# Retention heads with tokens on the partitions: GroupNorm along the free axis, the output transposed afterwards, and the samples' outputs as column tiles

## What is computed

```python
qf = rope(q), kf = rope(k) * DK ** -0.5            # DK 256, per head
scores = einsum('bhid,bhjd->bhij', qc, kc) * decay  # prompt tokens
inner = einsum('bhij,bhje->bhie', scores, vc)       # o of the prompt, 512 x 512 per head
S_new = S * chunk_dec + k^T v                       # state, 256 x 512 per head
...                                                 # samples: 8 states of their own, o_b = q_b S_new_b
mu = mean(o, axis=-1); var = mean(square(o - mu), axis=-1)
o = (o - mu) * rsqrt(var + EPS) * gn_gain           # GroupNorm over the 512 channels of a head
ret_branch = (silu(g_ret) * o) @ w_ret_out
```

## Time and profile before

| | |
|---|---|
| three runs | 2767.01, 2780.33, 2778.76 us; median 2778.76 |
| the profiled execution | span 2784.4 us |
| PE busy | 2598.1 us, 93% of the span |
| DVE, POOL, ACT busy | 1435.8, 1404.3, 594.0 us |
| mean granted TensorE clock | 0.964 of full |
| chain that ended last | PE 72%, DVE 14%, the rest waits between engines |

### The profile page before, as it was taken

The page is one execution under the profiler, slowest core; times in us unless marked ns, Lnnn a source line. Parts: engine busy times, 40 slices in busy tenths (PEclk is TensorE's granted clock), DMA queues, the critical chain, the costliest instruction groups (busy, mean ns, idle before and its releaser), DMA issues.

```text
span 2784.4 us, 53033 instructions
## 1 busy us (share of the span) xinstructions
PE 2598.1 (93%) x20388; PEld 2551.3 (92%) x20388; DVE 1435.8 (52%) x1644; ACT 594.0 (21%) x825; POOL 1404.3 (50%) x845
## 2 busy tenths in 40 slices
PE   7999999987889999999999999899888899999997
PEld 7998989987889989999998989898788899999997
DVE  6656454587764553223256453646876745431333
ACT  2303030316161121001112121213161611110111
POOL 4252526244456656666653525252455566566664
PEclk9999999999999999999999989999999999999999
DMA  4435353422222222232236252524222222222222
GB/s 156 168 122 164 121 160 118 159 72 68 65 78 89 92 76 92 86 96 91 88 131 199 89 189 91 191 92 163 62 73 72 74 92 89 76 89 93 91 87 87
DMA packets 113015, 298.52 MB, mean 107 GB/s; under 512 B 11681, under 2 KB 12449, under 8 KB 112865
## 3 DMA queue, kind: packets, MB, share of 16 engines
q1 hardware_dynamic: 60480, 199.78, 22.4%
q10 hardware_dynamic: 52384, 96.56, 10.4%
HBM read 255.92 MB, written 40.38 MB: 106 GB/s over the span
## 4 chain that ended last, share of the span: by engine, by line
PE 72%; DVE 14%; DVEq 7%; issue 3%; ACT 2%; ACTq 1%; DMA 1%; POOL 0%; POOLq 0%
PE proj L299 63%; PE aux L469 3%; DVEq L1011 2%; DVE scratch L829 2%; PE aux L460 1%; PE aux L450 1%; DVEq L828 1%; DVE scratch L775 1%; PE aux L417 1%; DVE scratch L913 1%; DVE scratch L917 1%; DMA scratch<-v_rows 1%; DVE scratch L780 1%; ACTq L1269 1%; DVE scratch L638 1%
## 5 line engine op out<-in xcount | busy, mean ns | idle before, releaser
L285 POOL TENSOR_SCALAR w_high<-w_raw 128x1024 fp32r<-128x1024 f32 (+3 forms) x420 | 438.0, 1043 | 1294.5 <-PE proj L299 1290.2
L287 POOL TENSOR_TENSOR w_low<-w_raw,w_high 128x1024 fp32r<-128x1024 f32 (+3 forms) x420 | 965.9, 2300 | 62.2 <-issue 1.5
L299 PE MATMUL proj<-x_high,w_high 128*128 128x260 f32 x4096 | 855.2, 291 | 97.0 <-DVE scratch L895 34.6
L299 PE MATMUL proj<-x_high,w_low 128*128 128x260 f32 x4096 | 841.5, 288 | 0.0
L299 PE MATMUL proj<-x_low,w_high 128*128 128x260 f32 x4096 | 840.4, 287 | 0.0
L299 PEld LDWEIGHTS proj<-x_high,w_high 128*128 128x128 f32 x4096 | 650.4, 194 | 109.9 <-issue 52.5
L299 PE MATMUL proj<-split_scratch,w_high 128*128 128x260 f32 x4000 | 655.4, 286 | 43.5 <-DVE scratch L802 17.1
L299 PEld LDWEIGHTS proj<-x_high,w_low 128*128 128x128 f32 x4096 | 648.3, 193 | 0.0
L299 PEld LDWEIGHTS proj<-x_low,w_high 128*128 128x128 f32 x4096 | 647.7, 193 | 0.0
L299 PEld LDWEIGHTS proj<-split_scratch,w_high 128*128 128x128 f32 x4000 | 556.4, 191 | 51.0 <-DVE scratch L802 18.3
L299 PE MATMUL proj<-split_scratch,w_low 128*128 128x260 f32 x2000 | 406.2, 285 | 0.0
(11 more groups left out here) (142 smaller groups left out, 2086.5 us busy)
## 6 DMA issues: line engine op xcount, KB each, us to landing
w_raw<-in_wstream SPq DMA_DIRECT2D x252, 512.0 KB, 3.3
scratch<-in_sret ACTq DMA_DIRECT2D x64, 512.0 KB, 6.3
out_ret_s<-scratch ACTq DMA_DIRECT2D x64, 512.0 KB, 6.4
w_raw<-in_wstream SPq DMA_DIRECT2D x72, 448.0 KB, 3.2
w_raw<-in_wstream SPq DMA_DIRECT2D x48, 384.0 KB, 3.1
scratch<-v_rows ACTq DMA_DIRECT2D x64, 256.0 KB, 5.3
w_raw<-in_wstream SPq DMA_DIRECT2D x48, 320.0 KB, 2.9
out_ret_p<-scratch ACTq DMA_DIRECT2D x8, 512.0 KB, 3.1
```

The costliest lines, as they stand in the source:

```text
L285: pool.tensor_scalar(WH[:, j, w], WR[:, j, w], 1.0, 0.0, ALU.mult, ALU.add)
L287: pool.tensor_tensor(WL[:, j, w], WR[:, j, w], WH[:, j, w].bitcast(F32), ALU.subtract).then_inc(s["w_split"], 1)
L299: m = pe.matmul(out, wt[:, w, blk * P:(blk + 1) * P], x[xi], start=first and n == 0, stop=last and n == 2)
```

## The change

Within a head, o is now made token-major. `attend(i)` takes the scores as weights and v as the streaming operand, so the 128 tokens of block i stand on the partitions and the 512 channels on the free axis. ACT copies each block to `OT`. The GroupNorm sums are then sums along the free axis: DVE's `bn_stats` and `bn_aggr` give mean and variance of each token, ACT takes the root of five columns, and DVE normalises `OT` with two per-partition scalars. `out_by_channel` transposes the result back on PE, behind the first two q tiles of the next head, and `outs_gated` multiplies it with the gate straight out of PSUM. The matrix of ones, the centring, the squares and the 128x520 reciprocal are gone.

The samples' outputs are made in two rounds of four. Each sample's q stands alone in one column of a 32-column block of zeros (`QZ`); that block is the stationary operand, the state streams past it (512 columns), and the four samples of a round write four 32-partition quarters of one bank.

Around it the order changes: `ret_out` stands behind the v tiles, with `sample_v` (transposes of the samples' v) ahead of it; `sample_out(0)` follows `ret_out`, and `sample_out(1)` stands behind the last gate (in head 0 behind `gate(2)` and at the very end). DVE makes the states of the first round between the tiles of `ret_out`. Four x tiles instead of two come ahead of the layer's last `ret_out`, and their convolutions stand between its tiles. Each bank of `aux` has its own semaphore for being free. Cut to its core:

```diff
-X_EARLY = 2
+X_EARLY = 4
...
-BANK = [0, 1, 2, 3, 0, 1, 2, 3, 0, 1, 2, 0, 1, 2, 0, 1, 2]
+N_VS, N_SC, N_TK, N_TV, N_AT, N_ST, N_OS, N_OT = 0, 1, 5, 7, 11, 15, 17, 18
+BANK = [0, 1, 2, 0, 1, 2, 0, 1, 2, 0, 1, 2, 0, 1, 2, 0, 1, 3, 2, 0, 1, 2]
...
+                def out_by_channel(hh):
+                    pe.wait_ge(s["o_norm"], hh * (TT + 1) + (TT + 1))
+                    aux_begin(N_OS, hh)
+                    for e in range(VT):
+                        m = pe.transpose(AUX[:, BANK[N_OS], e * P:(e + 1) * P],
+                                         OT[:, TT, e * P:(e + 1) * P], ID[:])
+                    m.then_inc(s["aux_mm"], 1)
+                    for e in range(VT):
+                        aux_begin(N_OT + e, hh)
+                        for i in range(TT):
+                            m = pe.transpose(AUX[:, BANK[N_OT + e], i * P:(i + 1) * P],
+                                             OT[:, i, e * P:(e + 1) * P], ID[:])
+                        m.then_inc(s["aux_mm"], 1)
...
+                    def attend(i):
+                        aux_begin(N_AT + i, hh)
+                        for j in range(i + 1):
+                            at = ST_OFF[j] + (i - j) * P
+                            for n, (a, b) in enumerate(((STH, VH), (STH, VL), (STL, VH))):
+                                m = pe.matmul(AUX[:, BANK[N_AT + i], :], a[:, at:at + P], b[:, j, :],
+                                              start=j == n == 0, stop=j == i and n == 2)
...
+                    def sample_out(r):
+                        pe.wait_ge(s["q_wide"], hh + 1)
+                        pe.wait_ge(s["s_new"], hh * NS + (r + 1) * SRING)
...
+                        for d in range(KT):
+                            for j in range(SRING):
+                                b = SAMPLE[r * SRING + j]
+                                m = pe.matmul(AUX[j * QW:(j + 1) * QW, BANK_SO, :],
+                                              QZ[:, d, b * QW:(b + 1) * QW], SS[j][:, d, :],
...
-                    for e in range(VT):
-                        attend(e)
-                        sample_out(3 + e)
-                    final_state(0)
-                    sample_out(NS - 1)
-                    final_state(1)
-                    pe.wait_ge(s["gn_sum"], hh * 2 + 1)
-                    column_sums(tb, v0 + VT + T_MEAN, SUM)
-                    gate(2)
-                    pe.wait_ge(s["gn_sum"], hh * 2 + 2)
-                    column_sums(tb, v0 + VT + T_VAR, SUM)
+                    for i in range(TT):
+                        attend(i)
+                    for d in range(KT):
+                        final_state(d)
+                    if first:
+                        sample_out(1)
...
+                    rotate(0, QF)
+                    if not first:
+                        outs_gated(hh - 1)
...
+                            if m_ in (2, 3, 4, 6):
+                                new_state((2, 3, 4, 6).index(m_))
...
+                    for d in range(KT):
+                        final_state(d)
+                    dve.drain().then_inc(s["sf_full"], 1)
+                    if first:
+                        for n in range(SRING, NS):
+                            new_state(n)
+                    attended(TT)
+                    dve.drain()
+                    for i in range(TT + 1):
+                        dve.bn_aggr(MV[:, i, :], BST[:, i, :])
+                    dve.drain().then_inc(s["gn_var"], 1)
+                    dve.wait_ge(s["gn_sd"], hh + 1)
+                    dve.reciprocal(RS[:], RS[:])
+                    dve.drain()
+                    for i in range(TT + 1):
+                        ts(OT[:, i, :], OT[:, i, :], MV[:, i, 0:1], RS[:, i:i + 1], ALU.subtract, ALU.mult
+                           ).then_inc(s["o_norm"], 1)
...
+                    def next_states():
+                        act.wait_ge(s["so_mm"], hh * ROUNDS + 1)
+                        for r in range(SRING):
+                            act.wait_ge(s_st[r], hh * (16 * ROUNDS) + 32)
+                            load_state(SRING + r)
```

More of the change, by code:

```diff
@@ L476, in one_head @@
+                    sample_v()
+                    if not first:
+                        ret_out(hh, ub, QK + VT, tb, QK + VT)
+                        sample_out(0)
+                    pe.wait_ge(s["qk_low"], hh * 2 + 2)
+                    for j in range(TT):
+                        scores(j)
+                    gate(0)
+                    for i in range(TT // 2):
+                        k_by_token(i)
                     v_by_token(0)
-                    gate(0)
+                    gate(1)
@@ L502, in _ @@
                     one_head(head, False)
-                for t in range(X_EARLY):
+                for t in range(2):
+                    x_tile(0, t)
+                out_by_channel((layer + 1) * HEADS - 1)
+                for t in range(2, X_EARLY):
                     x_tile(0, t)
@@ new lines, in one_head @@
+                    if not first:
+                        og_split(hh - 1)
+                        dve.drain()
+                    dve.tensor_copy(GNC[:], CUR[:, bass.ds(head * VT + PC_GN, VT)])
+                    rotate(KT, KF)
+                    ts(KSC[:], KF[:, :, SEQ:TOK], DK ** -0.5, None, ALU.mult)
+                    v_tile(0)
+                    low(KL, KF, KH, DK ** -0.5, 2)
+                    for e in range(1, VT):
+                        v_tile(e)
+                    aux(N_VS)
@@ new lines, in one_head @@
+                    if first:
+                        for j in range(TT):
+                            score_low(j)
+                        dve.drain()
+                        gate(0)
+                    else:
+                        score_low(0)
+                        score_low(1)
+                        dve.drain()
+                        gate(0)
+                        score_low(2)
+                        score_low(3)
+                        dve.drain()
+                        new_state(SRING)
@@ L1130, in one_head, with load_state @@
[L1130 to L1138 removed]
+                    def load_state(n):
+                        act.dma_start(SS[n % SRING], state(sret, SAMPLE[n])).then_inc(s_ld[n % SRING], 16)
@@ new lines, in one_head @@
+                    act.dma_start(DEC[:], dec[bass.ds(head, 1)].rearrange("a p n -> (a p) n")
+                                  ).then_inc(s["dec_ld"], 16)
+                    for r in range(SRING):
+                        act.wait_ge(s_st[r], hh * (16 * ROUNDS) + 16)
+                        load_state(r)
+                    act.wait_ge(s["rope_done"], hh * 2 + 1)
+                    A(QH, QF, copy).then_inc(s["qk_high"], 1)
+                    if not first:
+                        ret_tail(hh - 1)
@@ L1345, in weight_units @@
                     n += 1
+            projections([off[i] + h * DK + j * P for i in range(2) for j in range(KT)]
+                        + [off[2] + h * DV + j * P for j in range(VT)])
+            if h:
+                ret_out(h - 1)
+            projections([off[3] + h * DV + j * P for j in range(VT)])
         wide = GT * P
```

541 lines of the change are left out of this document (273 added, 268 removed).

## The result

The changed kernel takes 2665.17 us (median of 4 runs, 2660.95 to 2667.27) against 2777.08 before: a ratio of 0.9603, 95% interval 0.9578 to 0.9629, 112 us or 4.0% faster. The forecast was 2722, its range 2675 to 2785.

What follows compares the result with a forecast made beforehand. The prediction took PE as the bound. Heads 1 to 3 gain 34.0 us a layer and head 0 loses 5.8: 28.2 a layer, 56.5 in two, span 2784.4 to 2728, median 5.6 lower, 2722 us; range 2675 to 2785.

Steps and rivals of the forecast that it cites:

- S, the samples' round: PE time of one round of four samples, 16 passes: 3.9 us, bounds 1.73 and 6.9; forecast's chance 0.45.
- quarters together: Rival: the four quarters of a samples' round run at the same time, 1.73 us a round, 2688 us; chance 0.24.
- The bank wait: Heads 1 to 3: PE stands 4.0 us for bank 2 before the fourth output transpose; bounds 2 and 5.6.
- The clock behind it: Heads 1 to 3: a clock drop after PE's stand for bank 2 loses 2.4 us a head; bounds 0 and 2.4.
- Head 0: Loses its cover, PE standing 12.8 us before the last samples' round: 103.5 against 97.76 us, 5.8 lost a layer.
- Head 1's first two tiles: Start of head 1: 2.4 us counted for a lower clock after the samples' round ending the head before.
- GroupNorm's chain hidden: Behind the last `final_state`: a chain of 8 to 9 us costs nothing, covered by two q tiles, 11.6 us.
- The wait for the last v tile: Ahead of `sample_v`: PE waits for DVE to read the last v tile, taken as 0.75 us.
- Tail: Layer's last stretch, 80.25 us, counted as unchanged; bounds 14.1 us gained and 8.7 lost a layer.
- serial round: Rival: the quarters of a samples' round run in a row, 6.9 us a round, 2771 us; chance 0.18.
- draining passes: Rival: passes of a samples' round also drain between each other, 9.5 us a round, 2811 us; chance 0.07.
- late second round: Rival: in heads 1 to 3 the second samples' round's states come late and stop DVE, then PE; near 2770, chance 0.06.

Runs made afterwards that it cites:

- one_quarter: The changed kernel with all four samples of a round written to the same 32-partition quarter of the bank, outputs mixed; 2747.77 us.
- by_quarter: The changed kernel with the same samples' matmuls written one sample after another, both state halves of each together; 2665.77 us.
- split_mid: The changed kernel with DVE splitting the gated output between its readings of the two k tiles instead of ahead of both; 2669.46 us.
- gated_first: The changed kernel with DVE gating the transposed output between its readings of the two q tiles; 2676.82 us.
- no_cover: The changed kernel with output transposes ahead of the next head's first q tile and the gating product ahead of q's rotation; 2713.32 us.
- old_form: The changed kernel with samples' outputs from the old products, state blocks as weights and one q column streaming, four samples in a row; 2831.89 us.

## Why the prediction was wrong

- **S, the samples' round: the step that failed.** The prediction let a matmul's two passes stand one behind the other and only the next quarter's first pass run beside the second: nine pass times, 3.9 us. "Nothing shows the overlap, nor forbids it" was true, but this choice between the ends was the wrong one: all four quarters run together, and 1.86 was measured, close to four pass times; `one_quarter` (6.99 in one quarter) and `by_quarter` (1.87 in the other order) confirm it. In the six rounds of heads 1 to 3 this is 12.2 us a layer; layer 0's head 0 had 3.2 and 3.6, at the lower clock in part or whole, against 3.9 and 6.3. Together 16 of the 31 us by which layer 0's gain was too small (58.8 measured, 28.2 forecast). The Trainium skill ("TensorEngine Tiling (Array Packing)", Key Properties) says that different tiles load and multiply in parallel; the round of 1.86 us agrees. The Trainium skill ("TensorE: Matmul & The Clock Gate", Part 3, The mechanism) says that a load overlaps a running matmul only when its row group differs; here it did not hold, since these loads share all 128 rows, and eight of them were done by 210.67 while the first four passes, begun at 210.51, still ran. The rival *quarters together* had this mechanism; its 2688 was still 23 too high, for the reasons that follow.
- **The bank wait: right place, wrong size.** 4.0 forecast, 2.15 measured, some 5 us a layer in three heads. The q rotation's last two products were priced 1.00 + 2.07 from group means; without GpSimd beside them they take 0.70 + 0.69, which is 1.7 of the 1.85 us. The Trainium skill ("SBUF — State Buffer", "SBUF: two separate sides") says that a DVE operation with two operands in SBUF and a GpSimd operation that reads SBUF keep each other out of a shared port; the rows agree, 0.69 alone and up to 2.90 beside L298. No run here took GpSimd's work away.
- **The clock behind it: mostly not there.** 2.4 a head forecast, with nothing as the other bound. In the changed kernel's trace the other bound was right in five heads of six, and in layer 0's head 3 the clock fell, about 1.7 us; 5 to 7 us a layer. The prediction leaned on waits of 2.84 us and 4.33 us and read no shorter one, though the trace of the kernel before holds waits near 2 us with either clock behind them (above). That most of the changed kernel's heads kept the clock is in part luck: in `split_mid` the same wait lost it in four of six. The 3.27 us of `gated_first` lost it in all.
- **Head 0: right in its mechanism.** Loss forecast, 5.8; measured 1.4. The wait stood where it was put, 11.2 us against 12.8 (bounds 9 and 16): the v row landed in 3.27, not 5.3. The rest is S, 3.6 in the last round against 6.3. Head 1's first two tiles, for which 2.4 had been counted, lost 0.7 to the clock.
- **GroupNorm's chain hidden: right.** From the last `final_state` to the last normalisation 6.4 us, 8 to 9 forecast, under two tiles of 11.8; `no_cover` shows what it costs uncovered. Three prices in it had no row: 2.5 us for aggregate, root and small reciprocal; in head 2 they take 1.0 together.
- **Missed:** DVE's backlog ahead of the k tiles, 0.93 to 0.96 us of idle in two of layer 0's three heads; in head 3, where PE ran at the lower clock ahead of it, it did not show. The forecast had said that behind the bank wait only q's low half was queued; the split of the gated output (5.6 us) was queued too, and the k tiles behind it. The wait for the last v tile took 0.87, not 0.75.
- **Tail: near enough.** 2.3 us gained a layer where none was counted, inside its bounds.
- The rivals of a serial round, of draining passes and of a late second round did not come. With a serial round the forecast said 2771; `one_quarter` measured 2748, so the terms beside S were some 23 us too dear in all, the same 23 as above.

## What to carry to other kernels

When one unknown price stands in a sum sixteen times, the range must reach the far end of that price together with the kinder bounds of the other terms, not the far end alone. Look at the shortest, the median and the longest of a group before its mean is used: a mean of two lengths is the length of nothing. And a wait inside a stretch in which another engine runs without a break is no gain to be had: two short waits can be dearer to join than to leave apart, because of the clock: 3.27 us in one piece lowered it in six heads of six, 2.15 and 0.93 apart in one of six.

## What the runs showed of the hardware

- Four fp32 matmuls with 32 columns of weights each, written to four 32-partition quarters of one bank, run at the same time: 16 passes of 512 columns in 1.86 us, against 6.99 in one quarter, 3.76 times. The order in which they are written made no difference (1.87).
- The clock can fall though the profile shows no idle time of PE: in `old_form` it falls to 0.50 within 64 one-column fp32 records in a row (9.9 us), while it stays at 1.00 over 16 passes of 512 columns in one quarter (6.99 us).
- The same idle time can be followed by either level of the clock: 2.14 to 2.15 us by 1.00 in five heads of the changed kernel and by 0.67 in one, and by 0.66 in four heads of six in `split_mid`. Idle of 0.93 to 0.96 us left it at 1.00 each time at a head's start; idle of 3.27 to 3.30 (`gated_first`) lowered the 5 us behind it to between 0.50 and 0.68 in six heads of six.
- A DVE product with two operands in SBUF took 0.69 us in the six executions without GpSimd's L298 beside it and 2.85 to 2.90 in the ten with it.
